# The first layer of a six-part model: modulation groups of 256 channels instead of 512, with four gate blocks and the channel transforms placed among them

## What is computed

```python
shift, scale, gate = split(silu(c) @ ada_w[0] + ada_b[0], 3)      # for ctx: c_ctx
h = rmsnorm(x, norm_g[0]) * (1 + scale) + shift
y = (fft2_real(h by groups of 512 channels) * silu(h @ w_gate)) @ w_out
x = x + gate * y
```

## Time and profile before

| | us |
|---|---|
| three runs | 3239.69, 3236.70, 3239.34 (median 3239.34) |
| the profiled execution | 3236.72 |
| its span, first to last instruction | 3235.0 |
| mean granted TensorE clock | 0.983 |
| PE, DVE, ACT, POOL busy | 3128.0 (97%), 2118.6 (65%), 1301.8 (40%), 163.6 (5%) |

### The profile page before, as it was taken

How to read it: one execution, slowest core, us unless ns; L and a number is a source line. 1 busy time by engine, 2 the same in 40 slices (tenths; PEclk the granted TensorE clock), 3 DMA queues, 4 the chain that set the end, 5 groups by cost and what they waited for, 6 DMA issues and landing times.

```text
span 3235.0 us, 44077 instructions
## 1 busy us (share of the span) xinstructions
PE 3128.0 (97%) x17440; PEld 2617.6 (81%) x17440; DVE 2118.6 (65%) x3651; ACT 1301.8 (40%) x2056; POOL 163.6 (5%) x252
## 2 busy tenths in 40 slices
PE   7899999999999999999999999999999999989998
PEld 4677777878888888878777889899899988968776
DVE  2377654687887855666568855555756566556897
ACT  3322322522232222232445554444444344435676
POOL 0100000100000000000100000001100200010001
PEclk8999999999999999999999999999999999989999
DMA  8757685344545445467357736456664433666897
GB/s 298 281 189 271 242 285 203 104 166 155 195 167 177 167 158 191 157 201 238 126 200 253 244 120 197 135 172 200 208 209 146 144 118 127 198 247 202 293 370 273
DMA packets 190718, 648.91 MB, mean 201 GB/s; under 512 B 21920, under 2 KB 30240, under 8 KB 190128
## 3 DMA queue, kind: packets, MB, share of 16 engines
q1 hardware_dynamic: 136016, 450.96, 40.5%
q10 hardware_dynamic: 49536, 178.28, 16.2%
q0 software_dynamic: 4960, 16.85, 1.5%
HBM read 628.19 MB, written 15.73 MB: 199 GB/s over the span
## 4 chain that ended last, share of the span: by engine, by line
PE 84%; DVE 7%; ACT 4%; DMA 2%; issue 1%; POOL 0%; ACTq 0%; SPq 0%; POOLq 0%; DVEq 0%
PE PS L466 13%; PE PS L468 13%; PE PS L467 13%; PE PS L563 6%; PE PS L565 6%; PE PS L564 6%; DVE WL L1926 3%; ACT WH L1271 2%; PE PS L1169 2%; PE PS L808 2%; DMA AR<-ada_p 2%; PE PS L1171 2%; PE PS L1170 2%; PE PS L643 1%; PE PS L866 1%
## 5 line engine op out<-in xcount | busy, mean ns | idle before, releaser
L1926 DVE TENSOR_TENSOR WL<-WR,WH 128x1024 fp32r<-128x1024 f32 (+1 forms) x644 | 779.9, 1217 | 552.9 <-ACT WH L1271 550.0
L1271 ACT ACTIVATE WH<-WR 128x1024 fp32r<-128x1024 f32 (+1 forms) x644 | 672.9, 1051 | 951.3 <-PE PS L468 574.4
L466 PE MATMUL PS<-HTH,WH 128*128 128x256 f32 (+1 forms) x2624 | 871.2, 332 | 0.3 <-DVE WL L1926 0.3
L468 PE MATMUL PS<-HTH,WL 128*128 128x256 f32 (+1 forms) x2624 | 857.7, 327 | 0.0
L467 PE MATMUL PS<-HTL,WH 128*128 128x256 f32 (+1 forms) x2624 | 857.5, 327 | 0.0
L466 PEld LDWEIGHTS PS<-HTH,WH 128*128 128x128 f32 x2624 | 499.7, 190 | 61.6 <-issue 14.8
L467 PEld LDWEIGHTS PS<-HTL,WH 128*128 128x128 f32 x2624 | 499.8, 190 | 42.9 <-issue 1.7
L468 PEld LDWEIGHTS PS<-HTH,WL 128*128 128x128 f32 x2624 | 499.7, 190 | 42.8
L563 PE MATMUL PS<-WH,HTH 128*128 128x512 f32 x1016 | 408.2, 402 | 3.6 <-DVE WL L1926 3.6
L565 PE MATMUL PS<-WH,HTL 128*128 128x512 f32 x1016 | 396.3, 390 | 0.0
L564 PE MATMUL PS<-WL,HTH 128*128 128x512 f32 x1016 | 395.6, 389 | 0.0
(11 more groups left out here) (419 smaller groups left out, 4027.5 us busy)
## 6 DMA issues: line engine op xcount, KB each, us to landing
WR<-ada_w SPq DMA_DIRECT2D x256, 512.0 KB, 4.6
AR<-ada_p SPq DMA_DIRECT2D x128, 512.0 KB, 6.6
WR<-m_vo ACTq DMA_DIRECT2D x64, 512.0 KB, 4.2
WR<-a_qz ACTq DMA_DIRECT2D x64, 512.0 KB, 4.7
WR<-n_m SPq DMA_DIRECT2D x64, 512.0 KB, 4.2
WR<-e_gu SPq DMA_DIRECT2D x53, 512.0 KB, 5.3
YT<-e_gu SPq DMA_DIRECT2D x51, 512.0 KB, 5.6
WR<-f_out ACTq DMA_DIRECT2D x32, 512.0 KB, 5.3
```

The lines of the kernel that those rows point to most:

```text
L466: e.matmul(ps[:, 0:n], wh[:, k, :], xh, start=c == 0, stop=False)
L468: i = e.matmul(ps[:, 0:n], wl[:, k, :], xh, start=False, stop=c == K - 1)
L1271: e.activation(WH[:, s % NP, 0:n_], place_of(plan["slot"][p])[:, 0:n_], ACT.Copy, scale=1.0).then_inc(*L.up(hi_done, ("hi", s)))
L1926: e.tensor_tensor(WL[:, s % NP, 0:n_], place_of(plan["slot"][plan["split"][s]])[:, 0:n_], WH[:, s % NP, 0:n_].bitcast(F32), ALU.subtract). ...
```

## The change

- `GP` 16 to 8: groups of 8 shares and 2 channel blocks (256 channels); 8 groups per layer. `NG0` 6 to 4: the chunks serve 4 gate blocks (12 matmuls, piece 128x512), and gate blocks 4 and 5 become ordinary gate steps.
- The channel transforms leave `F_ORDER` and lie among the chunks, as 8 half transforms of 24 matmuls with PSUM banks 4 and 5. One or two shares follow each 6 or 12 matmuls instead of lumps of 3 to 6.
- The norm of x is made as in later layers: VectorE sums the squares, and the reciprocal is of 128x4; ScalarE copies the spread result to `RS`. Half of group 0's shares lie ahead of the sums.
- For layer 0 VectorE writes both low halves of h; GpSimd's part and ScalarE's second result go.
- Slots: the two transform pieces hold slots 0 and 1 throughout, and the 16 chunk pieces share the two halves of slot 2.
- Layer 1's shares: 3 behind each of 16 steps, then 2 behind each of 8. `bg`: 2 at gate block 14 and at output blocks 0 to 9; none in dft steps. Layer 0's `gate` is finished in two halves, the second one due at output block 8.

Cut to its core:

```diff
-NG0 = 6
-GP = 16
+NG0 = 4
+GP = 8
...
-            return [*(("dft", g) for g in range(4)), ("mix", 0), ("mul", 0), ("mul", 1), ("gate", 6), ("mul", 2), ("mul", 3),
...
+            return [("mix", 0), *(("mul", n) for n in range(4)), ("gate", 4), ("gate", 5), ("mix", 1), ("mul", 4), ("mul", 5),
...
-        LATER[place_] = range(64 + at, 64 + at + (3 if k < 20 else 2))
+        LATER[place_] = range(64 + at, 64 + at + (3 if k < 16 else 2))
...
+    GATES0 = [0, 1, 2, *range(5, 18)]
+    DFT0 = (3, 4)
+    def ws(s):
+        return DFT0.index(s) if s in DFT0 else 2 if s < 18 else (s + 2) % NP
...
+            def chunk(c, n, turned=None):
...
+                for k, ps in enumerate(gates):
...
+                    if k % 2:
+                        some_shares(n)
+                        if k == 1 and turned is not None:
+                            turn_share(turned, side(turned))
+            def transform(g, p, n, turned=None):
+                tbs = (2 * p, 2 * p + 1)
+                banks = [bank(4 + tb % 2, ("dft", 0, g, tb)) for tb in tbs]
+                for q in range(2):
...
+                    for tb, ps in zip(tbs, banks):
...
+                        some_shares(n)
+                        if (q, tb) == (0, tbs[0]) and turned is not None:
+                            turn_share(turned, side(turned))
+            shares(0, range(4), side(0))
+            sums_of("x0", 512)
+            shares(0, range(4, 6), side(0))
+            rows_from("x0", 512)
+            shares(0, range(6, 8), side(0))
+            turn_share(0, side(0))
+            for u in range(8):
+                g = (u - 1) // 2
+                left += [(u + 1, m) for m in range(8)] if u < 7 else []
+                if u == 0:
+                    chunk(0, 2)
+                    chunk(1, 2)
+                    turn_share(1, side(1))
+                elif u % 2:
+                    chunk(2 * u, 1)
+                    transform(g, 0, 1)
+                    chunk(2 * u + 1, 1)
+                    if u == 7:
+                        transform(3, 1, 0)
+                else:
+                    transform(g, 1, 2, u)
+                    chunk(2 * u, 0, u + 1)
+                    chunk(2 * u + 1, 0)
```

ScalarE:

```diff
+        def first_norm():
+            root("x0", 512)
+            cut_to(2)
+            w.wait_ge(L.at(("full", ("rs", "x0"))))
+            e.activation(RS, place[("rs", "x0")][:], ACT.Copy, scale=1.0).then_inc(
...
+            for u in range(8):
+                adap_row(u)
+                if u % 2 and u > 1:
+                    transformed(0, (u - 3) // 2, (2, 3), 1)
+                for j in (2 * u, 2 * u + 1):
...
+                cut_to(GATES0[2 * u + 1] + 1)
+                if u % 2:
+                    transformed(0, (u - 1) // 2, (0, 1), 0)
+            for n in range(NG0):
+                gate(("gate", 0, n), 512, F_TMP[n % 2], [("gated", 0, n - 2)] if n >= 2 else [])
+            cut_to(19)
+            transformed(0, 3, (2, 3), 1)
+            cut_to(18 + NP)
```

VectorE:

```diff
+        def first_norm():
+            rstd("x0", 512)
+            cut_to(2)
...
+            for u in range(8):
+                mod_of(u)
+                for j in (2 * u, 2 * u + 1):
...
+                        late.append((m, j, a, b, v))
+                        if len(late) > 2:
+                            low(*late.pop(0))
+                cut_to(GATES0[2 * u] + 1)
+                for x in late:
+                    low(*x)
+                late.clear()
+                cut_to(GATES0[2 * u + 1] + 1)
...
-                some = {0: 1, 1: 2 + n % 2}.get(tag, 0) if n < 14 else 0
+                some = {0: 2 if n < 10 else 1, 1: 2 + n % 2}.get(tag, 0) if n < 14 else 0
...
+        for n in range(NB - 1):
+            square_sum("x0", n)
...
-                    bg(2 if n < 14 else 1 if n == 14 else 0)
+                    bg(2 if n < 15 else 0)
```

More of the change, by code:

```diff
@@ L570, in statistics, with sums_of @@
         def statistics(tag, n):
+            sums_of(tag, n)
+            rows_from(tag, n)
+        def sums_of(tag, n):
             ps = wrk(("stat", tag))
[L572 to L577, removed]
             r = RS if n == 512 else RA
@@ L657, in side, with some_shares @@
                 return lambda job: bank(6 + c % 2, job)
[L659 to L669, removed]
+            gates = [bank(n, ("gate", 0, n)) for n in range(NG0)]
+            weights(("first", 0), [I["f_gate0"][c] for c in range(3)])
+            weights(("dft", 0), halves(I["dft_d"]))
+            weights(("first", 0), [I["f_gate0"][c] for c in range(3, NB)])
+            left = []
+            def some_shares(n):
+                for _ in range(n):
+                    if left:
+                        c, m = left.pop(0)
+                        shares(c, [m], side(c))
+            def chunk(c, n, turned=None):
+                s = GATES0[c]
+                wh, wl = part_of(WH, s), part_of(WL, s)
                 w.wait_ge(L.at(("lo", s), ("h", 0, c)))
[L671 to L674, removed]
+                for k, ps in enumerate(gates):
+                    b = slice(128 * k, 128 * k + 128)
                     e.matmul(ps[:], wh[:, b], HH_[:, c, :], start=c == 0, stop=False)
@@ L677, in first_gates @@
                     i = e.matmul(ps[:], wl[:, b], HH_[:, c, :], start=False, stop=c == 15)
-                    names = ([("full", ("gate", 0, n))] if c == 15 else []) + ([("used", s)] if n == NG0 - 1 else [])
+                    names = ([("full", ("gate", 0, k))] if c == 15 else []) + (
+                        [("used", s)] if k == NG0 - 1 else [])
                     if names:
                         i.then_inc(*L.up(mm_done, *names))
-                if at < GC - 1 and more:
-                    shares(g + 1, range(*parts[at + 1]), side(g + 1))
@@ L1368, in adap_row, with transformed @@
                 *L.up(act_done, ("adrow", c), ("free", ("adr", c))))
[L1370 removed]
+        def transformed(tag, g, tbs, part=1):
             for tb in tbs:
@@ L1398, in fnet @@
             tbs = list(range(a0 // 128, b0 // 128))
-            modnorm(tag, before, cols, free)
             if tag == 0:
-                for n in range(NG0):
-                    gate(("gate", 0, n), 512, F_TMP[n % 2], [("gated", 0, n - 2)] if n >= 2 else [])
-                cut_to(plan[("dft", 0)][0] + NP)
+                first_norm()
+            else:
+                modnorm(tag, before, cols, free)
             for kind, n in F_ORDER(tag):
@@ L2030, in modnorm @@
             for j in range(NB):
-                if tag and j == 2:
+                if j == 2:
                     cut_to(plan["first"][tag] + NP)
                 keep_up(tag, j)
[L2034 to L2038, removed]
                 w.wait_ge(L.at(mod(tag, 1, j)))
```

163 lines of the change are left out of this document (95 added, 68 removed).

## The result

The changed kernel takes 3246.65 us (median of 10 runs, 3243.97 to 3250.9) against 3238.72 for the kernel before on the same chips: ratio 1.0027, 95% interval 1.0017 to 1.0037. It is slower by some 8 us where 12 us less was forecast. The profiled execution took 3249.39 us, its span is 3247.7.

What follows compares the result with a forecast made beforehand. PE work bounds the kernel, with slack only ahead of the transforms' end: 41 + 127.5 + 5.5 + 1 + 2.8 = 177.8 us, plus 21.8 and 1.1 is 200.7; mix 0 at 200.9 against 213.3, gain 12.4, so 3226 us, range 3212 to 3240.

Steps and rivals of the forecast that it cites:

- What bounds the kernel: Whole kernel: slack lies only ahead of the transforms' end (212.6 us); behind it time is PE work, so savings pass through.
- Parts 1 and 3: Early units: PE work with spread shares 127.5 us; bare waits 5.5 and 1 us, clock loss 2.8; transforms end at 177.8.
- The loss to the clock: Early stage: seven matmuls at the lower clock, 1.4 us each at the first chunk and chunk 2, 2.8 us together.
- The price of a single share: Early units: a share standing alone among matmuls costs 0.43 + 0.33 = 0.76 us of PE time.
- Part 2: Start of the kernel: first chunk begins at 41 us instead of 61.84, bounds 38 and 46.
- Part 4: Behind the transforms: gate blocks 4 and 5 add 21.8 us, places and turns 1.1; added half blocks hidden by PE.
- The sum: Up to mix 0: 200.9 us after against 213.3 before, a gain of 12.4 us; 3226 us for the kernel.
- The slower rival: Groups 2 to 7: the turn's chain is bare at every group; 3260 us, 3252 without the clock; 8 in 100.
- The late pieces: Start and half transforms with pairs: waits of 5 and 4 us for pieces, 17 us lost; put at 3238; 14 in 100.
- The fourth rival: Start: first chunk stays near 61.8 us as sums and shares queue on PE; 20 us go, 3246; 4 in 100.
- What would show it: Signs: right if first chunk near 41 and transforms over at 178 us; wrong if new PE gaps in gate or output blocks.

## Why the prediction was wrong, point by point

- *What bounds the kernel.* Right for the kernel before. "A saving ahead passes straight through to the end" was the error in short: it holds only if what was overlapped with the saved time finds another cover.
- *Parts 1 and 3, the units.* The transforms were forecast to end at 177.8 us and end at 181.06. The order and place of all waits were right: 4.4 us before chunk 2, and 0.17 us before each of chunks 6, 10 and 14 where 0.35 was forecast. PE around chunk 2 and around chunk 6:

```profile
54.12 0.61 PE L670 MATMUL PS<-SML,AR 128*128 128x4 f32 x4 [0.51 <-ACT AR L1450]
59.13 0.79 PE L696 MATMUL PS<-HTH,WH 128*128 128x512 f32 x1 [4.40 <-DVE WL L2006]
...
95.52 0.50 PE L696 MATMUL PS<-HTH,WH 128*128 128x512 f32 x1 [0.17 <-DVE WL L2006]
```

  The 3.3 us too much lie mostly in the two units that begin at the lower clock: unit 0 took 18.5 us (17.2 forecast, with its bare wait) and unit 1 19.2 (18.4). The loss to the clock, taken at 1.4 us each time, was mis-sized there: 13.0 us from the first chunk to the turn against 10.3 of work is 2.7, and unit 1 against unit 3 (17.3) is 1.9. In unit 0 the lower clock lasted beyond the first two shares in the changed kernel's profile (a pair took 1.94 us instead of 1.07); in the run with one half block it ended ahead of them, and the same unit took 17.3 us. Units 2 to 6 took 86.3 us (84.9 forecast), 0.3 us more each. The price of a single share was right. A piece of the timeline in unit 1:

```profile
64.75 0.64 PE L662 MATMUL PS<-AR 128*32 128x256 f32 x8
65.31 0.50 PE L719 MATMUL PS<-WH,HTH 128*128 128x512 f32 x1
65.65 0.39 PE L720 MATMUL PS<-WL,HTH 128*128 128x512 f32 x1
...
66.58 0.40 PE L721 MATMUL PS<-WH,HTL 128*128 128x512 f32 x1
66.90 0.64 PE L662 MATMUL PS<-AR 128*32 128x256 f32 x8
```

  Six matmuls and a share take 2.15 us (64.75 to 66.90) against 6 x 0.228 + 0.76 = 2.13, and the run with pairs puts a place at 0.34 us against 0.33. The page TensorEngine Tiling of the Trainium skill (Key Properties) spoke against the change here: a change of tiling mode drains TensorE. The trace agrees, with these 0.34 us a place; 40 places are some 13 us of the early stage, as the prediction counted.
- *Part 2, the start.* Forecast 41 us for the first chunk, measured 40.59. In part two errors met: the column sums began at 27.05 us instead of 28.2 and took 3.5 us instead of 2.6. Behind them the order and the times were as given: the spreading at 32.41 (32.7), the turn at 36.80 (37.3). The lower clock was there as forecast.
- *Part 4, what moves behind.* Here the prediction failed, in two sentences. The first, "The wait of 0.76 us for the first late pieces stays", became 2.9 us of waits (1.70 and 1.24) and then a stretch at the lower clock: 18.6 us from one lump of shares to the next where 12.6 is usual, 6 us lost in this execution. Listing these pieces first gave back 3.8 us by the medians. The second, "Per output block this adds one, 2.6 us ... Hidden by PE", counted the added half block as VectorE's work and as bytes, and both were hidden; what it did to SyncE's queue was not followed. The second half block of a block runs after that block's end, and the next pieces stand behind it. That cost 11.3 us, as undoing it alone shows, and as moving the entries alone shows (11.6). "Their transfers, 0.5 MB more, replace one `ada_p` piece" is also not so where it mattered: blocks 2 to 5 keep three pieces, and 7.8 of the 8.2 us that TensorE waits for `ada_p` in the output stage lie behind these blocks. The prediction had named the queue's order for gate block 4 and not for the output blocks.
- *A place count.* Two more gate steps with three shares each move six shares into the gate stage, 3.2 us against the 0.7 given, and out of the output stage again; this evens out.
- *The sum.* 32.3 us won ahead of mix 0 (213.3 - 181.06), 21.8 and 1.1 spent as forecast: 9.4 us would have been left. The gate and output stages lost some 18 us instead. With the losses removed by count and by order the gain is 7.6 us; with the shares in pairs as well it is 12.2. That this is nearly the 12.4 of the sum is luck: the sum had no pairs in it, and the early stage fell 3.3 us short of it. A slip besides: 3224.3 and 2.6 are 3226.9, not the 3226 forecast; it changes nothing in the account.
- *Rivals.* None was the right one. The slower rival had the turn's chain bare at every group; it was bare once, before chunk 2, and for 0.17 us at three more. The late pieces were considered only at the start and inside the units, where TensorE had no wait for them at all after 59 us. The fourth rival gave 3246, which is the time measured, by chance: its mechanism, a first chunk that stays near 61.8 us, did not occur (40.59). No rival put a wait behind mix 0.
- *What would show it.* "PE gaps in gate and output blocks where there are none now" was named as a sign of being wrong, and it was the one that came.

Behind the first layer the span was 2674.8 us before and 2678.7 after. The same stretch took from 2674.0 to 2681.2 in the eleven other profiles, with both kernels' code for it (2674.0, 2679.0 and 2681.2 in the three that are the kernel before there), so these 4 us lie within the scatter of executions.

## What to carry to other kernels

When work that runs beside a stage is moved, follow each queue that its entries share, not only its engine time and its bytes: here a half block of 2.6 us on VectorE, and 0.5 MB, cost nothing that can be measured, but the transfer listed behind it was asked for 7 us later and TensorE waited. An in-order queue with waits in it should list what a busy engine needs next ahead of what waits for a slower one. And a place between unlike matmul shapes has a price of its own; spread small work in pairs rather than singles when the waits allow it.

## What the runs showed that was not expected

- Waits in a row of shares brought TensorE's clock down: after 1.70 and 1.24 us of waits at 197 to 201 us it was granted the lower level for some 6 us. Stretches of the changed kernel, with the clock third from the end:

```profile
200.00:203.00 3.00, 1.98 (x10) 1.03 (x11) 2.29 (x4) 0.00 (x0) 0.00 (x0) 0.50 0.86 296
203.00:205.00 2.00, 2.00 (x6) 1.57 (x5) 0.00 (x0) 0.00 (x0) 0.00 (x0) 0.50 0.81 295
207.00:210.00 3.00, 3.00 (x14) 2.44 (x14) 0.00 (x0) 0.00 (x0) 0.00 (x0) 1.00 0.43 176
```

  So 2.9 us of waits cost 6 us of time. This is not a fixed factor: a single wait of 2.08 us at 441 to 443 us left the clock at 1.00. The page TensorE: Matmul & The Clock Gate of the Trainium skill (Part 1) names the two levels, 1.2 and 2.4 GHz; the trace agrees with a pitch of 0.43 us for matmuls of 512 columns right behind the wait at 59.13 us and 0.23 us at 65.65.
- In the early stage the transfers and the other engines had much room left: from 59 to 181 us TensorE was busy 121.4 of 122.0 us, the transfers kept up with single pieces and pairs alike, and ScalarE and VectorE were busy 33 and 37 us.
